# Expert gate and up products with the weights stationary in two 64-column tiles, and experts of 104 rows

## What is computed

```python
hid = silu(h @ w_gate[e]) * (h @ w_up[e])      # 1024 -> 512 inner channels
y   = sum over the two experts of weight[e] * (hid @ w_down[e])   # 512 -> 1024
```

## Time and profile before

| | |
|---|---|
| median of 3 runs | 1578.72 us (1576.02, 1578.72, 1584.24) |
| span of the profiled execution | 1581.7 us |
| the profiled execution's own time | not listed beside its span; only the run of 1584.24 us is longer than the span |
| TensorE matmul busy | 1373.4 us, 87% of the span |
| TensorE weight loads | 734.0 us, 46% |
| VectorE, ScalarE, POOL busy | 554.7, 221.4 and 105.1 us |
| mean granted TensorE clock | 0.915 |
| DMA | 207.60 MB, mean 131 GB/s |
| expert stage (first gather to last store) | about 1150 to 1535 us of the span |

### The profile page before, as it was taken

The page is one execution under the profiler, slowest core; times in us unless marked ns, Lnnn a source line. Parts: engine busy times, 40 slices in busy tenths (PEclk is TensorE's granted clock), DMA queues, the critical chain, the costliest instruction groups (busy, mean ns, idle before and its releaser), DMA issues. The chain is left out here.

```text
span 1581.7 us, 12961 instructions
## 1 busy us (share of the span) xinstructions
PE 1373.4 (87%) x4958; PEld 734.0 (46%) x4958; DVE 554.7 (35%) x1225; ACT 221.4 (14%) x465; POOL 105.1 (7%) x144
## 2 busy tenths in 40 slices
PE   3779999799998799999999998997279999999970
PEld 1446466354756445555544444445234444444430
DVE  2665833557423752222212323216301111011116
ACT  1111001100153221111110001012001011011102
POOL 2031000010013200000000000000200000000011
PEclk8689976899999799999999999997579999999995
DMA  9332110111211110100111223334948988888714
GB/s 311 108 104 26 56 53 18 53 17 37 107 31 47 32 57 0 54 35 19 53 53 54 80 80 153 124 126 167 326 130 307 347 305 303 320 328 303 284 60 180
DMA packets 93634, 207.60 MB, mean 131 GB/s; under 512 B 10036, under 2 KB 11636, under 8 KB 93572
## 3 DMA queue, kind: packets, MB, share of 16 engines
q1 hardware_dynamic: 82696, 174.48, 30.6%
q0 software_dynamic: 8576, 23.95, 5.4%
q10 hardware_dynamic: 2304, 8.39, 1.3%
HBM read 189.03 MB, written 15.68 MB: 129 GB/s over the span
## 5 line engine op out<-in xcount | busy, mean ns | idle before, releaser
L760 PE MATMUL banks<-wring,HT 128*128 128x512 f32 x480 | 220.7, 608 | 0.8 <-ACTq L349 0.8
L603 PE MATMUL banks<-wring,HT 128*128 128x512 f32 (+1 forms) x480 | 196.5, 571 | 1.1 <-ACT REG L1070 0.5
L900 PE MATMUL banks<-wring,REG 128*128 128x512 f32 x320 | 141.6, 603 | 2.5 <-PE banks L900 1.7
L603 PEld LDWEIGHTS banks<-wring,HT 128*128 128x128 f32 x480 | 92.7, 195 | 100.5 <-issue 97.6
L760 PEld LDWEIGHTS banks<-wring,HT 128*128 128x128 f32 x480 | 88.8, 193 | 101.3 <-issue 95.2
L987 PE MATMUL banks<-REG 128*128 128x512 f32 x256 | 114.0, 598 | 12.7 <-ACT REG L1240 12.7
L1006 PE MATMUL banks<-wring,HT 128*128 128x512 f32 x256 | 114.0, 604 | 0.9 <-DVE HT L1856 0.9
L1006 PE MATMUL banks<-REG,HT 128*128 128x512 f32 x256 | 111.2, 592 | 0.0
L900 PEld LDWEIGHTS banks<-wring,REG 128*128 128x128 f32 x320 | 61.4, 193 | 82.2 <-issue 81.0
L987 PEld LDWEIGHTS banks<-REG 128*128 128x128 f32 x256 | 47.3, 190 | 69.9 <-issue 60.7
L579 PE MATMUL banks<-ident,REG 128*128 128x128 f32 x250 | 45.7, 348 | 38.5 <-DVEq L1445 16.2
(11 more groups left out here) (342 smaller groups left out, 1441.0 us busy)
## 6 DMA issues: line engine op xcount, KB each, us to landing
REG<-w_down SPq DMA_DIRECT2D x16, 2048.0 KB, 12.3
wring<-w_in SPq DMA_DIRECT2D x12, 2048.0 KB, 8.1
wring<-w_gate SPq DMA_DIRECT2D x8, 2048.0 KB, 9.9
wring<-w_up SPq DMA_DIRECT2D x8, 2048.0 KB, 16.3
REG<-w_gate SPq DMA_DIRECT2D x8, 2048.0 KB, 9.8
REG<-w_up SPq DMA_DIRECT2D x8, 2048.0 KB, 15.9
wring<-w_ada SPq DMA_DIRECT2D x7, 2048.0 KB, 15.3
HT<-w_ada SPq DMA_DIRECT2D x4, 2048.0 KB, 12.7
```

Source lines behind the costliest of these rows:

```text
L603: last = mm(out[:, 0:cols], HT[:, k, P * t:P * t + P], w[:, k, 0:cols], start=k == 0, stop=k == KD - 1)
L760: last = mm(chan.bank(), HT[:, k, P * (i % NT):P * (i % NT) + P], gate[1][:, k, :], start=k == 0, stop=k == KD - 1)
L900: last = mm(out, x[:, k, P * t:P * t + P], w[:, k, :], start=k == 0, stop=k == 3)
```

## The change

Gate and up trade their operands. The weights become stationary, 128 channels x 64 inner channels at a time, in two column tiles that write PSUM partitions 0 to 63 and 64 to 127; the token columns move, 104 of them. The inner state then comes out with channels on the partitions, four blocks of 128 channels side by side in a bank, 104 columns each. VectorE writes it straight to `HIDT`, so the four hidden transposes, ScalarE's copy and their semaphores go. `CAP` becomes 104, so gathers, transposes, copies, down products' output and stores have 104 rows; a pass covers 104 tokens an expert, there are at most 7 passes, and the lists grow to 728 places an expert. SP asks for the gate weights after the gate products of expert n - 2 instead of after its up products.

```diff
-CAP = 128
-PASSES = T // CAP
+CAP = 104
+PASSES = -(-T // CAP)
+LISTED = CAP * PASSES
...
-    HID = r0.take(2, 512)
-    HIDT = r0.take(2, 512)
+    HIDT = r0.take(2, 4, CAP)
...
-    ZERO = r.take(NE * T // P, dt=I32)
+    ZERO = r.take(NE * LISTED // P, dt=I32)
...
         def weights_in(n, m, e, b):
+            at_least(sp, gate_full, n - 1)
+            sp.dma_start(WG[b], a["w_gate"][0][e].rearrange("(k p) c -> p k c", p=P)).then_inc(wg_in[b], 16)
             at_least(sp, up_full, n - 1)
-            sp.dma_start(WG[b], a["w_gate"][0][e].rearrange("(k p) c -> p k c", p=P)).then_inc(wg_in[b], 16)
             sp.dma_start(WU[b], a["w_up"][0][e].rearrange("(k p) c -> p k c", p=P)).then_inc(wu_in[b], 16)
             at_least(sp, dn1, n - 1)
...
             pe.wait_ge(hid_ready, n + 1)
-            at_least(pe, ht_ready, n)
-            for k in range(4):
-                last = nc.tensor.transpose(banks[:, 4, P * k:P * k + P], HID[:, b, P * k:P * k + P], ident[:])
-            last.then_inc(ht_full, 1)
-            pe.wait_ge(ht_ready, n + 1)
             pe.wait_ge(wd_in[b], 16 * m + 16)
             for half, (full, emptied) in enumerate(((dn0, out_d), (dn1, out_a))):
                 at_least(pe, emptied, n)
                 for k in range(4):
-                    last = mm(banks[:, 5 + half, :], HIDT[:, b, P * k:P * k + P], WD[b][:, k, 512 * half:512 * half + 512],
+                    last = mm(banks[0:CAP, 5 + half, :], HIDT[:, b, k, :], WD[b][:, k, 512 * half:512 * half + 512],
                               start=k == 0, stop=k == 3)
...
             for k in range(KD):
-                last = nc.tensor.transpose(banks[:, k // 4, P * (k % 4):P * (k % 4) + P], ROWS2[:, b, P * k:P * k + P], ident[:])
+                last = nc.tensor.transpose(banks[:, k // 4, CAP * (k % 4):CAP * (k % 4) + CAP], ROWS2[0:CAP, b, P * k:P * k + P],
+                                           ident[0:CAP, 0:CAP])
...
-                for k in range(KD):
-                    last = mm(banks[:, bank, :], COLS2[:, b, k, :], w[b][:, k, :], start=k == 0, stop=k == KD - 1)
+                for f in range(4):
+                    for k in range(KD):
+                        for half in range(2):
+                            last = mm(banks[64 * half:64 * half + 64, bank, CAP * f:CAP * f + CAP],
+                                      w[b][:, k, P * f + 64 * half:P * f + 64 * half + 64], COLS2[:, b, k, 0:CAP],
+                                      start=k == 0, stop=k == KD - 1)
...
         def act_end(n, m, e, b):
-            act.wait_ge(ht_full, n + 1)
-            at_least(act, dn1, n - 1)
-            A(HIDT[:, b, :], banks[:, 4, :], ACT.Copy).then_inc(ht_ready, 1)
             act.wait_ge(dn1, n + 1)
...
             act.wait_ge(gate_full, n + 1)
             at_least(act, hid_ready, n)
-            A(TH, banks[:, 2, :], ACT.Tanh, scale=0.5).then_inc(th_ready, 1)
+            A(TH[:, 0:4 * CAP], banks[:, 2, 0:4 * CAP], ACT.Tanh, scale=0.5).then_inc(th_ready, 1)
...
+            hid = HIDT[:, b].rearrange("p f t -> p (f t)")
             dve.wait_ge(th_ready, n + 1)
-            at_least(dve, ht_full, n - 1)
-            stt(HID[:, b, :], TH, 1.0, banks[:, 2, :], ALU.add, ALU.mult).then_inc(hid_step, 1)
+            at_least(dve, dn1, n - 1)
+            stt(hid, TH[:, 0:4 * CAP], 1.0, banks[:, 2, 0:4 * CAP], ALU.add, ALU.mult).then_inc(hid_step, 1)
             dve.wait_ge(hid_step, n + 1)
             dve.wait_ge(up_full, n + 1)
-            tt(HID[:, b, :], HID[:, b, :], banks[:, 3, :], ALU.mult).then_inc(hid_ready, 1)
+            tt(hid, hid, banks[:, 3, 0:4 * CAP], ALU.mult).then_inc(hid_ready, 1)
...
-                pool.indirect_dma_start(ROWS2[:, e % 2, :], None, scratch_h2,
-                                        bass.IndirectOffsetOnAxis(ap=IDX[:, e:e + 1].bitcast(U32), axis=0)).then_inc(g_in[e % 2], 16)
+                pool.indirect_dma_start(ROWS2[0:CAP, e % 2, :], None, scratch_h2,
+                                        bass.IndirectOffsetOnAxis(ap=IDX[0:CAP, e:e + 1].bitcast(U32), axis=0)).then_inc(g_in[e % 2], 16)
```

More of the change, by code:

```diff
@@ L320, in build @@
     gate_full, up_full, th_ready, hid_ready = sem("gate_full"), sem("up_full"), sem("gate_tanh"), sem("hidden_ready")
-    ht_full, ht_ready, dn0, dn1 = sem("hidden_transposed"), sem("hidden_columns_ready"), sem("down_half0_full"), sem("down_half1_full")
+    dn0, dn1 = sem("down_half0_full"), sem("down_half1_full")
     out_d, out_a = sem("expert_out_by_vector"), sem("expert_out_by_scalar")
@@ L436, in build @@
     scratch_out = nc.dram_tensor("scratch_out", (NE * CAP, D), F32).ap()
-    lists = nc.dram_tensor("token_lists", (NE * T, 1), I32).ap()
+    lists = nc.dram_tensor("token_lists", (NE * LISTED, 1), I32).ap()
     scratch_su = nc.dram_tensor("scratch_su", (T, 512), F32).ap()
@@ L530, in sp_pass @@
             for k in range(2):
-                sp.dma_start(IDX[:, 8 * k:8 * k + 8], lists.rearrange("(e r) o -> r (e o)", r=T)[bass.ds(CAP * r, CAP), 8 * k:8 * k + 8],
+                sp.dma_start(IDX[0:CAP, 8 * k:8 * k + 8], lists.rearrange("(e r) o -> r (e o)", r=LISTED)[bass.ds(CAP * r, CAP), 8 * k:8 * k + 8],
                              allow_slow_non_contiguous=True).then_inc(idx_in, 16)
@@ L1237, in act_end @@
         def act_end(n, m, e, b):
-            act.wait_ge(ht_full, n + 1)
-            at_least(act, dn1, n - 1)
-            A(HIDT[:, b, :], banks[:, 4, :], ACT.Copy).then_inc(ht_ready, 1)
             act.wait_ge(dn1, n + 1)
             at_least(act, out_wr[b], 16 * m)
-            A(OUT[:, b, 512:1024], banks[:, 6, :], ACT.Copy).then_inc(out_a, 1)
+            A(OUT[0:CAP, b, 512:1024], banks[0:CAP, 6, :], ACT.Copy).then_inc(out_a, 1)
             act.wait_ge(out_a, n + 1)
             act.wait_ge(out_d, n + 1)
-            act.dma_start(scratch_out.rearrange("(e p) c -> e p c", p=CAP)[e], OUT[:, b, :]).then_inc(out_wr[b], 16)
+            act.dma_start(scratch_out.rearrange("(e p) c -> e p c", p=CAP)[e], OUT[0:CAP, b, :]).then_inc(out_wr[b], 16)
         def act_begin(n, m, e, b, before):
@@ L1250, in act_begin @@
             at_least(act, up_full, n - 1)
-            A(COLS2[:, b, 4:8, :], banks[:, 1, :].rearrange("p (a b) -> p a b", a=4), ACT.Copy).then_inc(gt_a, 1)
+            A(COLS2[:, b, 4:8, 0:CAP], banks[:, 1, 0:4 * CAP].rearrange("p (a b) -> p a b", a=4), ACT.Copy).then_inc(gt_a, 1)
             if before:
@@ L1841, in _ @@
             red(rk, EQ, ALU.add)
-            done(stt(CIDX[:, :, k], e_, float(T), rk, ALU.mult, ALU.add))
+            done(stt(CIDX[:, :, k], e_, float(LISTED), rk, ALU.mult, ALU.add))
         dve.sem_inc(pos_ready, 1)
@@ L1850, in dve_end @@
             at_least(dve, out_wr[b], 16 * m)
-            cp(OUT[:, b, 0:512], banks[:, 5, :]).then_inc(out_d, 1)
+            cp(OUT[0:CAP, b, 0:512], banks[0:CAP, 5, :]).then_inc(out_d, 1)
         def dve_begin(n, m, e, b, before):
@@ L1855, in dve_begin @@
             at_least(dve, up_full, n - 1)
-            cp(COLS2[:, b, 0:4, :], banks[:, 0, :].rearrange("p (a b) -> p a b", a=4)).then_inc(gt_d, 1)
+            cp(COLS2[:, b, 0:4, 0:CAP], banks[:, 0, 0:4 * CAP].rearrange("p (a b) -> p a b", a=4)).then_inc(gt_d, 1)
             if before:
                 before()
+            hid = HIDT[:, b].rearrange("p f t -> p (f t)")
             dve.wait_ge(th_ready, n + 1)
-            at_least(dve, ht_full, n - 1)
-            stt(HID[:, b, :], TH, 1.0, banks[:, 2, :], ALU.add, ALU.mult).then_inc(hid_step, 1)
+            at_least(dve, dn1, n - 1)
+            stt(hid, TH[:, 0:4 * CAP], 1.0, banks[:, 2, 0:4 * CAP], ALU.add, ALU.mult).then_inc(hid_step, 1)
             dve.wait_ge(hid_step, n + 1)
             dve.wait_ge(up_full, n + 1)
-            tt(HID[:, b, :], HID[:, b, :], banks[:, 3, :], ALU.mult).then_inc(hid_ready, 1)
+            tt(hid, hid, banks[:, 3, 0:4 * CAP], ALU.mult).then_inc(hid_ready, 1)
         def dve_pass(r):
```

## The result

The changed kernel takes 1524.01 us (median of 4 runs, 1521.92 to 1528.28) beside 1577.53 us for the kernel before: a ratio of 0.9657, 95% interval 0.9631 to 0.9683. A second, longer comparison gave 0.9634 (0.9612 to 0.9657). The forecast was 1522.5, with 0.964 as its ratio.

The account below looks back on a forecast made before the run. TensorE's chain was taken to bound the expert stage: cycles of 19.7 against 23.20 us save 52.5 over 15, the first gate/up 2.4, the end 1.4; 56 in sum, median 1522.5 us, range 1513 to 1545.

Parts of the forecast that it names:

- What bounds it: Expert stage: an expert costs what its TensorE chain costs, 23.20 us a cycle before; DMA keeps up.
- G: An expert's gate and up matmuls on TensorE: 13.73 us before, 11.5 forecast at 89.7 ns a pair of halves.
- Seams and T: Entering and leaving the two-tile form, 0.1 to 0.5 us an expert; leaving seam 0.16 plus transposes 0.87, together 1.03.
- T: Eight TensorE transposes of an expert's gathered rows: forecast to stay at 0.87 us and cover the wait for the hidden state.
- What goes, and the new wait: Hidden transposes and copy go, 1.3 to 1.7 us; down matmuls then wait for VectorE's hidden state, ready after 1.0 us.
- D: An expert's sixteen down matmuls on TensorE, 7.10 to 7.13 us before, forecast to keep sixteen instructions with 512 moving columns.
- First G and tail: Stage ends: first gate and up matmuls 16.70 to 14.25 us, saving 2.4; last down matmuls start earlier, saving 1.4.
- One: Rival: TensorE's longer loop code no longer stays on the engine, branches back cost 10 to 17 us, 1533 to 1539; chance 0.15.
- Two: Rival: weight loads of the halves run in series, 112 ns a pair, cycle 22.5 us, 1567 us; chance 0.05.
- Three: Rival: DMA becomes the bound, with 17.9 us of transfers a cycle; 1533 or 1569 us; chance 0.06.
- Four: Rival, slower: halves do not overlap while accumulating over eight k, 179 ns a pair, cycle 31.2 us, 1704 us; chance 0.05.
- Five: Rival: an expert gets more than 104 rows, so a second pass of some 330 us runs, 1850 us; chance 0.01.

Follow-up runs that it names:

- halves in turn: Changed kernel with all eight k of one 64-column half issued before the other half's, instead of alternating halves: 1639.72 us, ratio 1.037 to the kernel before.
- full-width run: Changed kernel with weights stationary as 128 columns in one piece, 104 token columns moving, 128 instructions an expert instead of 256: 1568.85 us, ratio 0.992.

## Why the prediction was right, point by point

**What bounds it**: right. The chain stayed on TensorE throughout.

**G**: 11.5 us forecast, 11.57 measured with its entry, from a row of another stage with other columns. 11.57 / 128 = 90.4 ns a pair, 89.7 forecast; in the stream a pair takes 89.2, and the entry makes up the rest. The halves in turn show that the overlap is the reason. The upper bound of a pair (112 ns, from L620) named a real limit, but that of one 128-column load; two 64-column loads in two tiles do not add up to it. The Trainium skill's rule in "TensorE: Matmul & The Clock Gate", section on LDWEIGHTS, columns / 1.2 in ns, gives 107 for 128 columns; the full-width run shows 112, so there it nearly holds. That section does not say whether the loads of two tiles run in series; read so, it would give 107 a pair too, and the pair of 90 ns contradicts that reading.

**Seams and T**: forecast 1.03 us for seam and T, measured 0.86. The prediction kept T at 0.87 for its 128 stationary columns; but with 104 moving ones the eight transposes take 0.71 us, as the full-width run shows, where no seam is ahead of them. So 0.15 of the 0.86 is the seam, near the 0.16 forecast, and it is T's 0.87 that was too long, by 0.16. The entry to G is inside its 11.57. T is most of the gap between 19.7 and 19.52 a cycle, 2.7 us in all.

**What goes, and the new wait**: right. D follows T directly, with VectorE's product done 0.16 us ahead of T's end (1229.46 and 1229.62), where the forecast saw next to nothing to spare; at the end, where no T covers it, VectorE's product stands for 0.60 us ahead of D (1463.30), as forecast.

**First G and tail**: 14.25 forecast and 14.34 measured, with the clock rising some 5.6 us in (1161.7, from the window's 0.64); the last D starts 0.7 us after G, 0.8 forecast.

**Rivals.** One did not occur, for a reason that no row of before could show, and its price of 10 to 17 us was too low by more than three times, by the estimate of 55 from the longer loop. Two fell with the full-width run and the pair of 89 ns. Three did not occur, but the term behind it was mis-sized: 17.9 us of transfers a cycle measured 20.0 in the run with half the channels, because the 399 GB/s of a 16 us burst was taken as a rate that holds; over eight cycles in a row it is 362. What makes the difference is open, beyond the part of the gathered rows. It stayed without effect since the up weights land 16.5 us or more ahead of their use in the changed kernel. (The 16.3 us taken there for the slowest landing is a median; the slowest of the up weights in the expert stage of before took 16.7, which changes nothing.) Four is excluded by the run of the changed kernel; the halves in turn show part of what it would have cost, a G of 18.47 us where no overlap at all would be 22.8. Five did not occur: one pass runs.

**Size**: 56 us forecast, 59 in the stage by the profile, 54 and 55 between the medians.

## What to carry to other kernels

Search the trace for the same instruction form in another stage before bounding it from afar: 64-column pairs elsewhere gave the new price to within 1%. When a stationary f32 operand changes with every 100 or so moving columns, its load can be the pace; here two 64-column tiles alternating in program order hid it, and in blocks of sixteen instructions they gave most of that away. After a gain on TensorE, look at the sum of transfers over a whole cycle and at the length of the loop's code: here both were nearer to deciding than the profile of before let see.

## What the runs showed of the hardware that was not expected

- The engine runs some three instructions ahead into the other half when halves come in blocks of sixteen (18.47 us instead of 22.8), so instructions of two tiles do not start in program order there (1252.44 ahead of 1252.71).
- A transpose's 128-column stationary is no bound at 112 ns: T with 104 moving columns takes 0.71 us in the full-width run (L992, 1241.94), 89 ns each, while f32 products with the same stationary width take 112 there.
- TensorE's code: 1,120 matmuls and loads a loop turn stay, 2,240 do not, and then each branch back costs about 11 us (the branch itself 6.1 against 0.22). The Trainium skill, "Runtime: NRT & Kernel Launch", section Instruction fetch mechanics, gives TensorE room for 2,048 instructions, which agrees; its window of two pages (512 instructions) for taken branches does not.
- Gathered rows cost over twice their share of the bytes when DMA is full: 20.04 us a cycle with them, 17.46 with almost none (one run).
- Transfers that take longer than a cycle stay hidden for many experts: with 100 rows the lead of the up weights falls from 19.8 to 7.5 us in twelve cycles, and no wait shows in the time.
